# Feed-forward down projection of an encoder block: seven products over operand quarters, through a ring of eight slots

## The reference

```python
u = rmsnorm(x, norm_ffn_g[l])
up = u @ w_up[l]
a = dwconv(up[..., :D_FF], ffn_conv_w[l], ffn_conv_b[l])
x = x + (jax.nn.gelu(a) * up[..., D_FF:]) @ w_down[l]
...
return rmsnorm(x, norm_final_g)
```

## Time and profile before

| | |
|---|---|
| median of 3 runs | 2665.56 us (2662.15 to 2666.32) |
| the profiled execution | 2663.53 us |
| its span, first to last instruction | 2661.9 us |
| TensorE clock granted, mean | 0.996 of full speed |
| window stage (18 windows) | 2068.23 to 2410.94 us |
| down projection, first to last matmul's start | 2414.17 to 2653.42 us |

### The profile page before, as it was taken

One profiled execution on the slowest core, in us unless ns is written; L12 is line 12 of the kernel. 1 busy time (PEld: TensorE's weight loads), 2 busy tenths in 40 slices (PEclk: granted clock), 3 DMA queues, 4 the chain that ended last, 5 costly groups with the idle time before them and its releaser, 6 DMA issues. The chain is left out here.

```text
span 2661.9 us, 37128 instructions
## 1 busy us (share of the span) xinstructions
PE 2621.7 (98%) x14980; PEld 2302.5 (86%) x14980; DVE 1490.3 (56%) x1762; ACT 866.0 (33%) x1022; POOL 449.0 (17%) x434
## 2 busy tenths in 40 slices
PE   7999999999999999999999999999999999999998
PEld 7888899999999999988888889977898888887887
DVE  5511100278888888554444424423348888887777
ACT  6321211234343334322223422333233434332111
POOL 3000000021122212332331001100011443430000
PEclk9999999999999999999999999999999999999999
DMA  8322232233332333434343535112212221224222
GB/s 275 121 99 95 95 119 89 93 104 103 111 102 95 102 110 102 150 119 151 126 150 130 204 125 206 32 48 79 72 64 95 101 90 65 94 80 182 104 103 79
DMA packets 166289, 297.04 MB, mean 112 GB/s; under 512 B 6971, under 2 KB 123015, under 8 KB 166176
## 3 DMA queue, kind: packets, MB, share of 16 engines
q1 hardware_dynamic: 108960, 137.13, 15.6%
q0 software_dynamic: 23248, 83.84, 9.3%
q10 hardware_dynamic: 33968, 74.52, 7.3%
HBM read 212.26 MB, written 83.20 MB: 111 GB/s over the span
## 5 line engine op out<-in xcount | busy, mean ns | idle before, releaser
L1299 DVE TENSOR_TENSOR wlo<-raw,whi 128x2048 fp32r<-128x2048 f32 x88 | 201.8, 2293 | 433.0 <-ACT whi L784 432.5
L1906 PE MATMUL ps<-whi,a_hi 128*128 128x256 f32 x1536 | 440.6, 287 | 0.5 <-DVE a_lo L1641 0.5
L1906 PE MATMUL ps<-wlo,a_hi 128*128 128x256 f32 x1536 | 435.1, 283 | 0.0
L1906 PE MATMUL ps<-whi,a_lo 128*128 128x256 f32 x1536 | 435.0, 283 | 0.0
L1875 PE MATMUL ps<-a_hi,whi 128*128 128x512 f32 x864 | 347.6, 402 | 0.2 <-DVE a_lo L1318 0.2
L1875 PE MATMUL ps<-a_hi,wlo 128*128 128x512 f32 x864 | 336.9, 390 | 0.0
L1875 PE MATMUL ps<-a_lo,whi 128*128 128x512 f32 x864 | 336.5, 390 | 0.0
L1906 PEld LDWEIGHTS ps<-whi,a_hi 128*128 128x128 f32 x1536 | 295.1, 192 | 1.4 <-DVE a_lo L1641 0.7
L1906 PEld LDWEIGHTS ps<-wlo,a_hi 128*128 128x128 f32 x1536 | 295.4, 192 | 0.4 <-issue 0.2
L1906 PEld LDWEIGHTS ps<-whi,a_lo 128*128 128x128 f32 x1536 | 295.1, 192 | 0.0
L789 ACT ACTIVATE ev<-ps 128x512 f32<-128x512 f32 x208 | 124.4, 598 | 508.5 <-PE ps L1875 290.3
(11 more groups left out here) (337 smaller groups left out, 5110.5 us busy)
## 6 DMA issues: line engine op xcount, KB each, us to landing
raw<-in_w_in SPq DMA_DIRECT2D x45, 1024.0 KB, 5.2
raw<-in_w_up SPq DMA_DIRECT2D x22, 1024.0 KB, 5.1
hg_T<-ev ACTq DMA_DIRECT2D x24, 512.0 KB, 2.7
qfb<-hg_T POOLq DMA_DIRECT2D x24, 512.0 KB, 5.0
hidden_T<-ga ACTq DMA_DIRECT2D x11, 1024.0 KB, 4.0
raw<-in_w_down SPq DMA_DIRECT2D x11, 1024.0 KB, 7.0
s<-hidden_T SPq DMA_DIRECT2D x11, 1024.0 KB, 4.9
raw<-in_w_kv_x SPq DMA_DIRECT2D x8, 1024.0 KB, 6.4
```

Of the source, the lines that this page charges most:

```text
L1299: signal(dve, dve.tensor_tensor(wlo[:, b.slot], w4[:, b.slot], whi[:, b.slot], ALU.subtract), w_lo, b.count())
L1906: ins = pe.matmul(ps[:, u, part * BC:(part + 1) * BC], op[sw][:, k, t * P:(t + 1) * P], W[mw][:, b.slot, k], start=k == 0 and q == 0, stop ...
```

## The change

The down projection is made by the same kind of scheme as the windows. Per group, the hidden block is seen as quarters a(token half, channel half), each 128 channels by 512 tokens, and the 256 rows of `w_down` as quarters b(channel half, column half), each 128 by 512. Seven products replace eight. Product i is summed over all 11 groups in PSUM (four banks of 128 tokens each, two sets in turn) before the next begins, so there are 77 steps p of 12 matmuls. The left and right operand of each step (128 x 512 each, 256 KB each) are read from DRAM into one of eight slots: `ring_a` stands where `s2` and `s3` were, `ring_b` where `a_hi` was. A slot's low part overwrites its raw data. The four sums of `w_down`'s quarters are made by POOL early in the kernel, for all 11 groups, and written to DRAM. The four sums of each hidden group are made by POOL from `ga` during the window stage (`hidden_sums`) and written to DRAM. The products are put together by DVE (`down_out`) in three buffers that stand where `a_lo` was, and then in `res`. The residual is loaded in one piece.

```diff
+LEFT = ("a11", "s2", "s3", "a12", "s1", "s4", "a22")
+RIGHT = ("b11", "t2", "t3", "b21", "t1", "b22", "t4")
+RING = 8
+N_DOWN = PRODUCTS * NFF
...
+        hsum_d = dram("hidden_sums", [NFF, 4, P, HALF])
+        wsum_d = dram("down_weight_sums", [NFF, 4, P, HALF])
...
-            def hidden_load(g):
-
-                sp.wait_ge(h_put, 16 * g + 16)
-                if g < 2:
-                    sp.wait_ge(unit_done, product(N_WIN - 1, 1 + g))
+            def down_load(p):
+
+                i, g = divmod(p, NFF)
+                if p >= RING:
+                    sp.wait_ge(f_dn, p - RING + 1)
                 else:
-                    sp.wait_ge(f_dn, 16 * (g - 1))
-                src = hidT_d[g * BC:(g + 1) * BC, :].rearrange("(k p) t -> p k t", p=P)
-                sp.dma_start(h_raw[g % 2], src).then_inc(ya_ld[g % 2], 16)
-
-            for g in range(NFF):
-                b = Blk(B_DOWN + g)
-                sp.wait_ge(w_lo, b.count(-2))
-                rows_ = A["w_down"][0][g * BC:(g + 1) * BC, :]
-                sp.dma_start(raw_dn[:, b.slot], rows_.rearrange("(k p) n -> p k n", p=P)).then_inc(w_ld[b.slot], 16)
-                hidden_load(g)
+                    sp.wait_ge(unit_done, product(N_WIN - 1, 2 if p < 4 else PRODUCTS - 1))
+                l, r = LEFT[i], RIGHT[i]
+                if l[0] == "a":
+                    sp.wait_ge(h_put, 16 * g + 16)
+                    k, t = int(l[2]) - 1, int(l[1]) - 1
+                    left = hidT_d[(2 * g + k) * P:(2 * g + k + 1) * P, t * HALF:(t + 1) * HALF]
+                else:
+                    sp.wait_ge(sum_io, 32 * NFF + 16 * g + 16)
+                    left = hsum_d[g, int(l[1]) - 1]
+                if r[0] == "b":
+                    k, c = int(r[1]) - 1, int(r[2]) - 1
+                    right = A["w_down"][0][(2 * g + k) * P:(2 * g + k + 1) * P, c * HALF:(c + 1) * HALF]
+                else:
+                    sp.wait_ge(sum_io, 32 * NFF)
+                    right = wsum_d[g, int(r[1]) - 1]
+                for side, src in enumerate((left, right)):
+                    sp.dma_start(slot("raw", p)[:, side], src).then_inc(slot_ld[p % RING], 16)
+
+            for p in range(N_DOWN):
+                down_load(p)
...
+
+            def quarter_sums(x11, x12, x21, x22, dst, first):
+
+                terms = ((x21, x22, ALU.add), (dst[:, 0], x11, ALU.subtract), (x11, x21, ALU.subtract), (x12, dst[:, 1], ALU.subtract)) if first else \
+                    ((x12, x11, ALU.subtract), (x22, dst[:, 0], ALU.subtract), (x22, x12, ALU.subtract), (x21, dst[:, 1], ALU.subtract))
+                for i, (x_, y_, op) in enumerate(terms):
+                    ins = pool.tensor_tensor(dst[:, i], x_, y_, op)
+                    if i < 3:
+                        line(ins)
+                return ins
+
+            for g in range(NFF):
+                pool.dma_start(wd[:], A["w_down"][0][g * BC:(g + 1) * BC, :].rearrange("(k p) n -> p k n", p=P)).then_inc(sum_io, 16)
+                pool.wait_ge(sum_io, 32 * g + 16)
+                line(quarter_sums(wd[:, 0, 0:HALF], wd[:, 0, HALF:D], wd[:, 1, 0:HALF], wd[:, 1, HALF:D], wd_sums, False))
+                pool.dma_start(wsum_d[g].rearrange("i p n -> p i n"), wd_sums[:]).then_inc(sum_io, 16)
+                pool.wait_ge(sum_io, 32 * g + 32)
+
+            pool.wait_ge(st[0], 16 * 13)
+            pool.wait_ge(st[1], 16 * 12)
 
...
+            def hidden_sums(g):
+
+                pool.wait_ge(f_mul, g + 1)
+                dst = s4[:] if g else wt[:].rearrange("p i k n -> p i (k n)")
+                if g == 1:
+                    pool.wait_ge(op_lo, 4 * KT + 4)
+                ins = quarter_sums(ga[:, 0, 0:HALF], ga[:, 1, 0:HALF], ga[:, 0, HALF:T], ga[:, 1, HALF:T], dst, True)
+                signal(pool, ins, s_t, hidden_sum(g))
+                pool.dma_start(hsum_d[g].rearrange("i p n -> p i n"), dst).then_inc(sum_io, 16)
+                pool.wait_ge(sum_io, 32 * NFF + 16 * g + 16)
+
+            hidden_sums(0)
+            weight_sums(0)
             for n in range(N_WIN):
...
+                if n + 1 < N_WIN:
+                    weight_sums(n + 1)
+                if n % 2 == 0:
+                    hidden_sums(PLAIN + n // 2 - 1)
+            hidden_sums(NFF - 1)
+            pool.wait_ge(a_st, 64)
+            pool.wait_ge(unit_done, product(N_WIN - 1, PRODUCTS - 1))
             pool.wait_ge(s_ev, PRODUCTS * N_WIN)
-            residual(2, 6, 2)
+            pool.dma_start(res[:], x3_d.rearrange("(t p) n -> p t n", p=P)).then_inc(x_ld[0], 16)
             pool.dma_start(gfin[:], A["norm_final_g"].rearrange("(a n) -> a n", a=1).to_broadcast([P, D])).then_inc(acc_ld, 16)
...
+                    act.wait_ge(s_t, hidden_sum(PLAIN + n // 2 - 1))
...
+            def down_hi(p):
+
+                act.wait_ge(slot_ld[p % RING], slot_base[p % RING] + 32 * (p // RING) + 32)
+                signal(act, act.activation(slot("hi", p), slot("raw", p), ACT.Copy), f_hi, p + 1)
+
+            def final_sq(t):
+
+                act.wait_ge(f_acc, t + 1)
+                signal(act, act.activation(ga[:, t % 2], res[:, t], ACT.Square, accum_out=ss[:, 1, t:t + 1]), n_sq, 26 + t + 1)
...
+            for p in range(2, N_DOWN):
+                if p == 4:
+                    hidden_store(NFF - 1)
+                down_hi(p)
+                i, g = divmod(p, NFF)
+                if i == PRODUCTS - 1 and 5 <= g < 9:
+                    final_sq(g - 5)
+            for t in range(4):
+                store(t)
+            for t in range(4, NT):
+                final_sq(t)
+                if t >= 6:
                     store(t - 2)
             store(NT - 2)
...
+                    dve.wait_ge(s_t, hidden_sum(0))
...
+                if final:
+                    down_lo(0)
...
+                if final:
+                    down_lo(1)
...
+                dve.wait_ge(f_dn, NFF * (i + 1) + (t if i == PRODUCTS - 1 else 0))
+                bank, read = ps[:, down_bank(i, t)], PRODUCTS * N_WIN + 4 * i + t + 1
+                m1_, u2_, u3_ = [combo(b, t) for b in range(3)]
+                low, high = [res[:, k + t, :] for k in (0, 4)]
+                add = lambda d, x_, y_: dve.tensor_tensor(d, x_, y_, ALU.add)
+                if i >= 3 and t == 0:
+                    dve.wait_ge(x_ld[0], 32)
+                if i == 0:
+                    signal(dve, dve.tensor_copy(m1_, bank), s_ev, read)
+                elif i == 1:
+                    signal(dve, add(u2_, m1_, bank), s_ev, read)
+                elif i == 2:
+                    signal(dve, add(u3_, u2_, bank), s_ev, read)
+                elif i == 3:
+                    signal(dve, add(m1_, m1_, bank), s_ev, read)
+                    line(add(low[:, 0:HALF], low[:, 0:HALF], m1_))
+                elif i == 4:
+                    line(add(u2_, u2_, bank))
+                    signal(dve, add(m1_, u3_, bank), s_ev, read)
+                    line(add(high[:, HALF:D], high[:, HALF:D], m1_))
+                elif i == 5:
+                    signal(dve, add(u2_, u2_, bank), s_ev, read)
+                    signal(dve, add(low[:, HALF:D], low[:, HALF:D], u2_), f_acc, t + 1)
+                    line(add(high[:, 0:HALF], high[:, 0:HALF], u3_))
+                else:
+                    signal(dve, add(high[:, 0:HALF], high[:, 0:HALF], bank), f_acc, 4 + t + 1)
 
             def final(t):
 
...
-            hidden_lo(0)
+            down_lo(2)
+            down_lo(3)
             gated(NFF - 1)
-            for g in range(NFF - 1):
-                down_adds(g, range(2))
-                split_lo(Blk(B_DOWN + g + 1))
-                down_adds(g, range(2, 8))
-                hidden_lo(g + 1)
-                down_adds(g, range(8, 16))
-            dve.wait_ge(acc_ld, 16)
-            for t in range(NT):
-                down_adds(NFF - 1, (2 * t, 2 * t + 1))
+            for p in range(4, N_DOWN):
+                down_lo(p)
+                i, g = divmod(p, NFF)
+                if i and 3 <= g < 7:
+                    down_out(i - 1, g - 3)
+                if i == PRODUCTS - 1 and g == 7:
+                    dve.wait_ge(acc_ld, 16)
+                if i == PRODUCTS - 1 and g >= 8:
+                    final(g - 8)
+            final(3)
+            for t in range(4):
+                down_out(PRODUCTS - 1, t)
                 if t:
-                    final(t - 1)
+                    final(3 + t)
             final(NT - 1)
...
+            def down_pe(p):
+
+                i, g = divmod(p, NFF)
+                pe.wait_ge(f_lo, p + 1)
+                for t in range(4):
+                    bank = down_bank(i, t)
+                    if g == 0:
+                        if i == 0:
+                            pe.wait_ge(s_ev, PRODUCTS * (N_WIN - 1) + (1, 2, 3, 5)[t])
+                        elif i == 1:
+                            pe.wait_ge(s_ev, PRODUCTS * N_WIN)
+                        else:
```

(69 more changed lines are left out.)

66 lines of the change are left out of this document (22 added, 44 removed).

## The result

The changed kernel takes 2634.48 us (median of 4 runs, 2633.57 to 2636.50), against 2665.62 us before (2662.15 to 2666.32): a ratio of 0.9884, 95% interval 0.9872 to 0.9895. The forecast was 2637.3, the range 2633.5 to 2648. The profiled execution took 2634.17 us, its span is 2632.6.

The account below looks back on a forecast made before the run. PE's step from matmul to matmul was taken as the bound; -29.9 (matmuls) - 3.4 (gap) + 4.0 (tail) + 0.5 (step 4) + 0.5 (entry) = -28.3 us, from 2665.56 to 2637.3 us, range 2633.5 to 2648.

Parts of the forecast that it names:

- The matmuls: Down projection: 924 PE matmuls instead of 1056, at 0.2268 us each, 29.9 us less.
- The gap: PE's 3.23 us wait for low parts before the down stage disappears: 3.4 us less, counted start to start.
- The tail: After the last matmul: four token tiles complete 0.68 us apart and queue for adds and scalings, 4.0 us more (2.5 to 6).
- The two allowances: 0.5 us more each, for the down projection's step 4 and for the entry to the window stage.
- the entry: Start of the window stage: DVE 3 to 4.5 us late beside POOL's sums, against 3.9 slack; 0.5 us (0 to 3).
- step 4: Fifth down-projection step, loaded only after the windows' last product: low part after 8.1 us against 10.9; 0.5 us (0 to 2).
- The ring: Down projection's eight-slot operand loads: load, copy and subtraction take 7.1 us within 19.0 us of lead; cost nothing.
- the residual load: Down stage: one 4 MB load, first read 90 us in, takes queue rate for some 20 us; hidden.
- this rival: Windows: POOL's hidden sums push DVE or POOL's chain past 38.1 us per pair, PE waits; 2646 to 2651 us, chance 0.14.
- The ring's rival: Down projection: a step's loads do not overlap, 5.0 us per step, 175 us more, about 2812 us; chance 0.07.
- the fourth rival: Down projection: DVE falls behind at seven changes of product, 3 us each, 2655 us; chance 0.05.
- The early sums of the weights: POOL, early in the kernel: eleven rounds of 16 to 21 us inside a 214.61 us wait; cost nothing.

Follow-up runs that it names:

- eight products: Changed kernel with the first product done once more ahead of the seven, in banks not read (88 steps, 1056 matmuls): 2664.94 us, ratio 1.0002.
- the tail by tiles: Changed kernel with the token tile as outer loop in the last four steps of the down projection: 2630.99 us, ratio 0.9864.

## Why the prediction was right

**The matmuls, -29.9.** Right: 924 at the same step, and eleven steps put back cost 30.5.

**The gap, -3.4.** The size is right, and so is that PE had waited for a low part. The reason given is only half of it. DVE's timeline, before and then after:

```profile
2411.05 0.69 DVE L1763 TENSOR_TENSOR ev<-u,ps 128x512 f32<-128x512 f32 x1 [1.96 <-PE ps L2319]
2411.78 2.29 DVE L1828 TENSOR_TENSOR s_lo<-s,s_hi 128x2048 fp32r<-128x2048 f32 x1
```

```profile
2407.30 1.22 DVE L1909 TENSOR_TENSOR down_lo_a<-down_raw_a,down_hi_a 128x1024 fp32r<-128x1024 f32 x1
```

Before, the weight split was done at 2405.5 and ACT's copy of the hidden block at 2405.0, but the hidden split stood behind the add of the last product in DVE's order: DVE was idle for 1.96 us and could not begin it. In the changed kernel the first two low parts stand ahead of the adds of the last two products, and the first is ready at 2408.52, 2.5 us ahead of PE. The prediction named the narrower split and the early loads. The loads are needed, as the run without them shows; of the order and the width no run separates the two, but 2.29 us begun at 2409.1, after the adds before the idle time, would have ended at 2411.4, against a next step at 2410.8: by this estimate the order alone is worth 2.7 of the 3.4 us.

**The tail, +4.0.** 12.4 - 8.5 = +3.9. The predicted order of adds and scalings is the one in the trace; the last scaling starts at 2628.06, 7.8 us after the last matmul's start, where 7.7 was worked out.

**The two allowances, +0.5 each.** Both are nothing. Of the entry: the first factor was ready at 2067.44, 3.1 us later than before, as predicted (3 to 4.5), and PE took it at 2068.47; 1.0 us of the slack was left. Of step 4: its low part runs from 2418.80 to 2420.73, 1.93 us beside POOL's last sums, and is needed at 2421.91: the allowance was not needed, by a us.

**The sum.** -29.9 - 3.4 + 3.9, and the windows beginning 0.2 us later (2068.47 for 2068.23), are -29.2, against 2663.53 - 2634.17 = 29.4 for the profiled executions. The medians lie 31.1 apart, since before's is 2.1 us above its profiled execution and after's 0.3; the forecast had carried 2.0 over. That, which is scatter and not mechanism, and the allowances are why the result is at the low end of the range.

**The ring.** Costed at nothing, and right: no wait of PE on a low part, 2.9 us to landing in the median, copies of 1.06 and subtractions of 1.23 us. The Trainium skill, "DMA: Bandwidth & Descriptors" (Rules for kernel authors, and Anatomy of one DMA), asks for 1 MiB or more per DMA for the most bandwidth; its fixed cost plus bytes, given there for DMAs issued from GpSimd, gives an estimated 2.6 us for one of 256 KB. The trace agrees with that for a single load, though these are issued from SP: 2.4 us at the least, 2.6 in the median for those of the hidden block in the steady state. But loads in one queue overlapped, and here four times smaller ones cost nothing at all. Two sentences of the prediction were too easy. One says that two 256 KB loads cannot take longer than 4.9 us: the eight issued from 2400.34 on took 4.1 and 5.0 in the medians, being queued behind each other, and some beside the residual load far more; the lead of 10.9 us covered the first. The other is on the residual load, "which seven steps of lead absorb": they do, by 0.4 us at step 16. With eight products and with the tail by tiles the same load made PE wait 0.6 and 0.5 us, and issued 17.6 us earlier in the stage, as without the sums, it cost 4 us.

**The rivals.** The windows do not pay for the sums: without them nothing is gained. The slack of "1 to 3 us per pair" was 2.9 to 3.8 on GpSimd's chain, but this rival was nearer than a slack suggests: two operations more per block, 2.9 us, and the kernel is 16 us slower than the changed one. DVE's subtractions beside POOL's operations took up to 1.7 us, not 1.2 to 1.4; in seven pairs they cost DVE 13.6 us more (94.8 for 81.2, two of them by the cut of the window), and its convolutions, now less often beside the weight sums, 5.9 less (54.8 for 60.7). That second term, which the prediction did not have, kept DVE under 38.1 us. The ring's rival was far: it takes a quarter of the lead to get there, 5.3 us per step and 6% slower than before. Of the fourth rival: there are six changes of product and not seven. The early sums of the weights began 39 us into POOL's long wait, at 176.68, and took 17.1 us a round, within the 16 to 21 given; `load_q` came at 365.09 for 352.55, and its first use at 489.37 as before. At the changes of product PE never waited.

## What to carry to other kernels

When PE sets the time and never waits, matmuls taken out are worth their number times its step, if the work that feeds the rest can be put where other engines wait; check each such place for its slack, and count in it the landing of every store that the engine waits for. Look also at the order of each engine's queue at a change of stage: here work for the next stage stood behind a wait for the last. A deep ring is sized by its worst neighbour and not by its steady state: one large load on another queue stretched small loads to 15 to 20 us, so look for what else is issued in the first round of a ring, and hold it back. In a last reduction step, order the matmuls so that output tiles complete as far apart as their epilogue is long.

## What the runs showed of the hardware

- Beside a 4096 KB load on POOL's queue, the slowest 256 KB load on SP's queue took 15.6 us to land in the changed kernel, 16.65, 16.84 and 20.08 in three of the others, and 9.4 at the least in any, instead of 2.4 to 3; the large one took 21.4.
- A 1024 KB store and a 1024 KB load that met took 8.2 and 7.0 us, instead of 4.9 and 5.1.
- After 6.28 us without work PE came back at 1.2 GHz for about 4 us (granted clock 0.50, matmuls 0.43 us apart). With an idle time of about 3 us every second step the granted clock was 0.82 to 0.83 throughout, and twelve matmuls took 4.42 us instead of 2.72; after a single one of 3.23 us it was 1.00.
- DVE and POOL, both on SBUF: the Trainium skill's "SBUF — State Buffer" (Who interferes with whom) has them lock each other out, and the trace agrees: DVE's subtractions took 0.69 us alone and mostly 1.0 to 1.7 beside POOL's operations. In a pair of windows DVE's busy time grew by 1.2 us in the mean, not the 2.8 allowed for, and in one by 3.5.
